# A decoder layer on one core: the expert blocks' tokens gathered from rows sorted once, in eight chunks, in place of a gather in every block

## What is computed

```
logits = rmsnorm(h) @ w_router + b_router          # 32 experts
top_v, top_e = top_k(logits, 4); gates = softmax(top_v)
for every expert e, x = the rows of rmsnorm(h) routed to e:
    gu   = x @ w_gate_up[e] + b_gate_up[e]          # 1024 -> 2048
    gate = min(gu[:, :1024], 7); up = clip(gu[:, 1024:], -7, 7)
    y    = ((up + 1) * gate * sigmoid(1.702 * gate)) @ w_down[e] + b_down[e]
    out[token] += gates[token, e] * y
```

## Time and profile before

| | us |
|---|---|
| median of 3 runs | 1140.28 (1140.24 to 1141.91) |
| profiled execution, its own time | 1138.94 |
| its span | 1137.1 |
| TensorE busy | 1101.7 (97%) |
| VectorE busy | 272.4 (24%) |
| ScalarE busy | 154.3 (14%) |
| moved by DMA | 427.34 MB, mean 376 GB/s |

### The profile page before, as it was taken

The page is one execution under the profiler, slowest core; times in us unless marked ns, Lnnn a source line. Parts: engine busy times, 40 slices in busy tenths (PEclk is TensorE's granted clock), DMA queues, the critical chain, the costliest instruction groups (busy, mean ns, idle before and its releaser), DMA issues.

```text
span 1137.1 us, 13236 instructions
## 1 busy us (share of the span) xinstructions
PE 1101.7 (97%) x5236; PEld 448.5 (39%) x5236; DVE 272.4 (24%) x623; ACT 154.3 (14%) x285; POOL 8.0 (1%) x28
## 2 busy tenths in 40 slices
PE   9999989999999999998999999999999999999997
PEld 7855755533333333333333333333333333333332
DVE  3643344421111111122111111111111111111111
ACT  3531323510000000010000000000000000000001
POOL 1000000000000000000000000000000000000000
PEclk9999998999999999999999999999999999999999
DMA  9593112899999999999999999999999999999996
GB/s 328 100 364 156 74 75 79 353 400 397 429 426 429 427 430 428 436 427 428 427 431 433 428 430 433 429 432 430 429 435 428 426 432 431 432 433 423 428 427 249
DMA packets 37329, 427.34 MB, mean 376 GB/s; under 512 B 6163, under 2 KB 8308, under 8 KB 17460
## 3 DMA queue, kind: packets, MB, share of 16 engines
q1 hardware_dynamic: 34724, 426.33, 89.7%
q10 hardware_dynamic: 2576, 0.59, 0.2%
HBM read 424.29 MB, written 2.62 MB: 375 GB/s over the span
## 4 chain that ended last, share of the span: by engine, by line
PE 80%; DMA 15%; ACT 2%; DVE 2%; issue 1%; SPq 0%; POOL 0%; ACTq 0%; DVEq 0%; POOLq 0%
PE bank L1677 31%; PE bank L1723 17%; DMA store<-in_w_gate_up_dram 8%; DMA store<-in_w_down_dram 7%; PE bank L1298 5%; PE bank L1619 4%; PE bank L1421 4%; PE bank L1305 4%; PE bank L1492 3%; PE bank L1369 2%; PE bank L1665 2%; PE bank L1608 2%; ACT conv L788 1%; PE bank L1685 1%; PE bank L1239 1%
## 5 line engine op out<-in xcount | busy, mean ns | idle before, releaser
L1677 PE MATMUL bank<-store,conv 128*64 128x512 f32 x2048 | 447.8, 595 | 1.5 <-DMA store<-in_w_gate_up_dram 1.5
L1677 PEld LDWEIGHTS bank<-store,conv 128*64 128x64 f32 x2048 | 144.1, 137 | 303.9 <-issue 296.9
L1723 PE MATMUL bank<-store,conv 128*64 128x512 f32 x1008 | 224.2, 595 | 5.9 <-DMA store<-in_w_down_dram 5.4
L1162 DVE TENSOR_SCALAR conv<-bank 128x512 f32<-128x512 f32 x32 | 22.1, 692 | 641.2 <-PE bank L1677 641.2
L1723 PEld LDWEIGHTS bank<-store,conv 128*64 128x64 f32 x1008 | 70.7, 137 | 137.7 <-issue 127.5
L782 ACT ACTIVATE conv<-conv 128x512 f32<-128x512 f32 x32 | 20.1, 629 | 497.6 <-DVE conv L1162 497.6
L1421 PE MATMUL bank<-arena,qkT 128*64 128x512 f32 x256 | 62.2, 605 | 0.2 <-DVE qkT L975 0.2
L1619 PE MATMUL bank<-qkT 64*128 64x512 f32 x248 | 61.6, 615 | 0.0
L1298 PE MATMUL bank<-store 128*128 128x512 f32 x128 | 56.4, 592 | 0.0
L792 ACT COPY qkT<-bank 128x512 f32<-128x512 f32 x32 | 18.7, 585 | 255.6 <-PE bank L1723 255.6
L1305 PE MATMUL bank<-store 128*128 128x256 f32 x192 | 42.7, 380 | 0.8 <-DVE store L842 0.8
(11 more groups left out here) (289 smaller groups left out, 578.2 us busy)
## 6 DMA issues: line engine op xcount, KB each, us to landing
store<-in_w_gate_up_dram SPq DMA_DIRECT2D x38, 4096.0 KB, 24.9
store<-in_w_down_dram SPq DMA_DIRECT2D x62, 2048.0 KB, 17.7
store<-in_w_gate_up_dram SPq DMA_DIRECT2D x52, 2048.0 KB, 16.5
store<-in_w_in_dram SPq DMA_DIRECT2D x7, 2048.0 KB, 22.8
store<-in_w_out_dram SPq DMA_DIRECT2D x1, 4096.0 KB, 18.0
extra<-in_w_down_dram SPq DMA_DIRECT2D x1, 2048.0 KB, 19.4
store<-in_w_down_dram SPq DMA_DIRECT2D x2, 1024.0 KB, 34.6
bias_by_distance<-extra SPq DMA_DIRECT2D x1, 1536.0 KB
```

The source lines that it names most:

```text
L1162: dve.tensor_scalar(gt, bank[4][:], LIMIT, None, ALU.min).then_inc(g_min, 1)
L1677: ins = mm(dst[SLOTS * hf:SLOTS * (hf + 1), :], xgT[:, c:c + SLOTS], store[:, slot_at(k, odd) + c0:slot_at(k, odd) + c0 + 512], start=Fals ...
L1723: ins = mm(dst[SLOTS * hf:SLOTS * (hf + 1), :], turned[:, c:c + SLOTS], w[:, hf * 512:(hf + 1) * 512], start=f == 0, stop=f == KT - 1)
```

## The change

All 1024 routed rows are put into their experts' order once, in a buffer in SBUF (`flow`, which also holds `hx`, `extra` and the old `conv`), turned and scaled. A block then takes its 64 columns from an offset that is read from a table (`win_at`).

- The buffer is filled by eight chunks of 128 rows. For each, VectorE makes two 0/1 matrices of 128x128 (`choose`), and TensorE multiplies the tokens `h` with them: 2 x 8 products of 128 columns (`chunk_half`). VectorE scales each half into place (`sorted_rows`, writing every eighth element). Chunks 0 and 1 are made in blocks 0 and 1, chunks 2 to 5 in blocks 2, 4, 6 and 8. Chunks 6 and 7 are made in `late_tables`, by two times 8 products of 256 columns (`chunk_end`), and TensorE waits there until VectorE has put them in place.
- `turns(b)` loses `gather`, the copy to `xg`, `gather_flip` and the scaling by VectorE. ScalarE copies the block's columns from `flow` to `xgT` (`window`).
- Block 0's rows are gathered already turned, by 16 products of 64 columns, so that ScalarE's norm of `h`, its copy and the transposes before block 0 go. The factor 1/rms is put into `SEL` and the chunk matrices.
- Five small products (`offsets`) inside block 0's `gate_up` sum the experts' counts to offsets.
- VectorE's loop over blocks 0 to 9 is written out.
- SyncE loads block 2's first down half ahead of block 1's second.

```diff
             for hf in range(2):
-                    if (m, hf) == (1, 0):
+                    if (m, hf) == (2, 0):
                         continue
-                    sp.wait_ge(wdn_used, 1 if hf == 0 else 2 * m)
-                    sp.dma_start(tile_dst(4 + hf), expert_tile(slice(m, m + 1), 4 + hf)).then_inc(ld_tile[4 + hf], 16)
+                    e = m if hf else 2
+                    sp.wait_ge(wdn_used, 2 * m if hf else 1)
+                    sp.dma_start(tile_dst(4 + hf), expert_tile(slice(e, e + 1), 4 + hf)).then_inc(ld_tile[4 + hf], 16)
...
+            def window(b):
+                at8 = act.value_load(win_at[0:1, bass.ds(b, 1)], min_val=0, max_val=KT * S * TOP_K)
+                act.wait_ge(wgu_used, 4 * b)
+                act.copy(xgT.rearrange("p (i h s) -> p i h s", i=4, h=2),
+                         flow[:, bass.ds(at8, KT * SLOTS)].rearrange("p (s h i) -> p i h s", h=2, i=4)
+                         ).then_inc(xgT_ready, 1)
...
+            def choose(chunk, dst):
+                if chunk:
+                    st.step(dve.tensor_scalar(pos4, pos4, -float(P), None, ALU.add))
+                both(lambda t: dve.tensor_scalar(dst[t], iota_p[:], pos4[:, 4 * t:4 * t + 1], None, ALU.is_equal))
+                for k in range(1, TOP_K):
+                    both(lambda t: dve.scalar_tensor_tensor(out=dst[t], in0=iota_p[:],
+                                                            scalar=pos4[:, 4 * t + k:4 * t + k + 1], in1=dst[t],
+                                                            op0=ALU.is_equal, op1=ALU.add))
                 for t in range(T):
+                    cr.mark(dve.tensor_scalar(dst[t], dst[t], nrm[:, 1, 2 + t:3 + t], None, ALU.mult))
...
+            def sorted_rows(at, n, k0, ks, src):
+                xs.mark(dve.tensor_tensor(
+                    flow[:, KT * at:KT * (at + n)].rearrange("p (s k) -> p k s", k=KT)[:, k0:k0 + ks],
+                    src[:].rearrange("p (k s) -> p k s", k=ks), wide(w2p[:, k0:k0 + ks], n), ALU.mult))
...
+                if chunk is not None:
+                    dve.wait_ge(ch_psum, 2 * chunk + 1)
+                    sorted_rows(P * chunk, P, 0, 4, bank[6])
                 dve.wait_ge(actT_psum, b + 1)
                 dve.tensor_copy(actT_last if last else actT, bank[4][:]).then_inc(actT_ready, 1)
-                if not last:
-                    dve.wait_ge(xgT_psum, b + 2)
-                    turned_rows().then_inc(xgT_ready, 1)
...
+            def chunk_half(c, half):
+                if half == 0:
+                    pe.wait_ge(chosen_ready, T * c + T)
+                if not (isinstance(c, int) and (c, half) == (0, 0)):
+                    pe.wait_ge(xs_ready, 2 * c + half)
+                for i in range(4):
+                    for t in range(T):
+                        ins = mm(bank[6][:, i * P:(i + 1) * P], h_rows(t, 4 * half + i), chosen[t], start=t == 0,
+                                 stop=t == T - 1)
+                ins.then_inc(ch_psum, 1)
...
+                pe.wait_ge(tab_ready, 10)
+                chunk_end(range(4, KT))
+                pe.wait_ge(xs_ready, 16)
...
-            def turns(b):
+            def turns(b, chunk=None):
                 turn_gates(b)
-                pe.wait_ge(S_ready, b + T + 1)
-                gather(0)
-                gather(1).then_inc(xg_psum, 1)
+                if chunk is not None:
+                    chunk_half(chunk, 0)
                 turn_act(b)
-                pe.wait_ge(xg_ready, b + 2)
-                gather_flip()
...
-            def rest(b):
-                turns(b)
+            def rest(b, chunk=None):
+                turns(b, chunk)
                 down(b, 0)
+                if chunk is not None:
+                    chunk_half(chunk, 1)
                 down(b, 1)
```

More of the change, by code:

```diff
@@ L263, in hybrid_layer @@
         rmT = conv[0:N_EXP, HG + T:HG + 2 * T, 0:P]
-        more, end, beg = (col[0:N_EXP, c:c + 1] for c in (24, 25, 26))
+        more, end, beg, cnt, extra_at = (col[0:N_EXP, c:c + 1] for c in (24, 25, 26, 27, 28))
+        minus_one = col[0:N_EXP, 3:4]
+        within, beyond = (tables[:, 192 + P * i:192 + P * (i + 1)] for i in range(2))
+        win_of, jump = r3[:, 448:480], r3[:, 480:512]
+        at = [left[t][:, 0:N_EXP] for t in range(T)]
+        pos4 = nrm[:, 7, 8:16]
         bank = [ctx.enter_context(nc.psum_tensor(f"bank{i}", [P, 512], F32)) for i in range(8)]
@@ L796, in expert_block @@
                 evacuate(b)
+                window(b + 1)
                 output(b, bank[7])
-            with act.Fori(0, FINE_BLOCKS) as b:
-                expert_block(b)
+            act.wait_ge(pad_ready, 1)
+            act.wait_ge(win_ready, 1)
+            with act.Fori(0, FINE_BLOCKS // 2) as pair:
+                for i in range(2):
+                    gated(2 * pair + i)
+                    evacuate(2 * pair + i)
+                    act.wait_ge(xs_ready, 2 * pair + (2 * i + 2))
+                    window(2 * pair + (i + 1))
+                    output(2 * pair + i, bank[7])
             act.wait_ge(gT_psum, 1)
@@ L1145, in _ @@
             shares(1)
[L1147 to L1156 removed]
+            dve.wait_ge(cnt_psum, 1)
@@ L1198, in _ @@
                 (st.step if j < S // SLOTS - 1 else nb.mark)(ins)
+            for c in range(2):
+                choose(6 + c, [chosen_end[t][:, P * c:P * (c + 1)] for t in range(T)])
             dve.wait_ge(end_psum, 1)
@@ L1601, in _ @@
             keep_clock()
-            pe.wait_ge(hn_ready, T)
             pe.wait_ge(S_ready, T)
-            gather(1).then_inc(xg_psum, 1)
-            def gather_flip():
-                for c in range(4):
-                    last = tp(bank[6][:, c * P:(c + 1) * P], xg_rows[:, c], ident[:])
-                last.then_inc(xgT_psum, 1)
-            pe.wait_ge(xg_ready, 1)
-            gather_flip()
+            gather(1).then_inc(xgT_psum, 1)
+            for t in range(T):
+                ins = mm(bank[1][0:N_EXP, 64:65], mask[t], ones[:, 0:1], start=t == 0, stop=t == T - 1,
+                         skip_group_check=True)
@@ L1614, in combine, with chunk_end @@
+            def chunk_end(ks):
+                for k in ks:
+                    dst = bank[(6, 7, 4, 5)[k // 2]][:, (k % 2) * S:(k % 2 + 1) * S]
+                    for t in range(T):
+                        ins = mm(dst, h_rows(t, k), chosen_end[t], start=t == 0, stop=t == T - 1)
+                ins.then_inc(ch_psum, 1)
             def combine(first=False, final=False):
@@ L1625, in late_tables @@
             def late_tables():
-                for i in range(T):
-                    ins = mm(bank[4][0:N_EXP, 0:1], mask[i], ones[:, 0:1], start=i == 0, stop=i == T - 1)
-                Tally(pe, cnt_psum).mark(ins)
                 pe.wait_ge(gates_ready, T)
@@ L1680, in gate_up @@
                         ins.then_inc(wgu_used, 1)
+                    if first and k == 1:
+                        offsets()
             def turn_gates(b, dst=bank[7]):
```

168 lines of the change are left out of this document (106 added, 62 removed).

## The result

| | before | after |
|---|---|---|
| median, us | 1140.26 (4 runs, 1139.86 to 1141.91) | 1196.74 (4 runs, 1193.53 to 1198.51) |
| ratio | | 1.0489 [1.0464, 1.0514] |
| span of the profiled execution | 1137.1 | 1194.5 |

The change costs 56.5 us where the prediction had 24 and ended its range at 1176. The direction was right, the size was not.

What follows compares the result with a forecast made beforehand. The prediction held the weight stream nearly full and TensorE's arrival at block 12's load decisive. Its terms 0.8 + 1.1 + 11.1 + 2.8 - 3.5 + 11.5 gave +23.8 us, forecasting 1164 us, range 1154 to 1176.

Steps and rivals of the forecast that it cites:

- way into block 0: Ahead of block 0, turned gathers replace the copy and transposes but take longer: +0.8 us.
- `offsets`: In block 0, five small products at 0.22 us each: +1.1 us (0.6 to 1.4).
- six blocks with a chunk: Chunk halves between `down` halves add 11.1 us; those in `turns` replace the gather but wait on VectorE, +2.8.
- four blocks without: Blocks 3, 5, 7, 9: the gather goes but VectorE's chain stays, saving 0.9 us of 1.89 each: -3.5 us.
- `late_tables` and the pause: Behind block 9: `chunk_end` products +7.1 us, then TensorE's wait for four `sorted_rows` +4.4: +11.5 us (9.7 to 12.9).
- half clock in block 6 and behind the tables: Only behind `late_tables`: a longer TensorE pause at half clock may add 0.6 us; not counted in the sum.
- block 12's load: Issued behind `late_tables`; each microsecond TensorE reaches its releasing product later is one of the result: +23.8 us.
- The step that failed: Chunk halves: 16 records at 1.85 us despite weights read every fourth element; 2.8 each only as upper end.
- The rule that I weighed: Chunk products' weights: a stride up to 16 bytes, four fp32 elements, is free, so 1.85 us a half stays.
- moved load: Block 2's first down half, loaded earlier, fills the dent at 255 us, but the gap returns at block 12's load: 0.
- the gather had been cover: In blocks without a chunk, the removed gather mostly covered VectorE's chain: only 0.9 us saved of 1.89.
- new wait: Rival: in blocks 0 and 1 `window` waits for the chunk's second half, or VectorE stalls: 1180 us, chance 0.10.

Runs made afterwards that it cites:

- unit rows: Changed kernel with token rows read side by side, weights left as they were, so the output differs: 1165.87 us, ratio 1.0230.
- experiment 2: Small program with only groups of 16 products or transposes at several weight pitches; 128 columns: 3.76 us at pitch 2, 7.36 at pitch 4.
- pitch-2 kernels: Changed kernel with rows of h paired, so product weights have a stride of 2 elements: 1172.74 us; the same without chunks 6 and 7: 1161.8 us.
- experiment 5: Kernel before with 28 idle products added ahead of block 10: 1148.04 us; or added behind block 27 instead: 1149.26 us.

## Why the prediction was wrong

Its sum and what the trace of after has, from the starts of `gate_up` (L1797: 237.75, 271.85, 305.62, 339.47, 366.10, and so on) against those of before:

| term | summed | measured |
|---|---|---|
| way into block 0 | +0.8 | 237.75 - 230.50 = +7.2 |
| `offsets` | +1.1 | +1.0 |
| six blocks with a chunk | +11.1 + 2.8 = +13.9 | 6 x 6.3 = +37.7 |
| four blocks without | -3.5 | 4 x -0.9 = -3.6 |
| `late_tables` and the pause | +11.5 | 25.7 - 13.9 = +11.8 |
| half clock in block 6 and behind the tables | 0 | 1.6 + 1.3 = +2.9 |
| block 12's load | +23.8 | +57.0 (timeline 57.2) |

- **The step that failed** is "I keep 1.85 since the records of L1608 still follow each other closely, and the ratio for the upper end". A chunk half takes 3.84 us on the average, and each gather 3.7 to 3.8. Six halves between the `down` halves and six in `turns` are 12 x 2.0 = 24 us above the sum; the second kind was summed as lying in the gather's place, which holds only at 1.85. Against the kernel with unit rows the two gathers add 3.7 us and their half clock about 2.0; the other 0.8 of the way into block 0 was missing from the sum without any pitch. The half clock in block 6 adds 1.6, `chunk_end` 0.8. L1608 was a bad witness: it is a transpose, one record, and in experiment 2 a transpose at this pitch costs 9% more, two records of a product of 128 columns twice as much. Why a transpose's load is the shorter one no run shows.
- **The rule that I weighed** was read too quickly, and the row that spoke against it, the longer load of L1608, was set aside. The Trainium skill (SBUF — State Buffer, "Door 1: The DMA port swizzle") says that a stride is free up to four fp32 elements, and in the same place that at least two accesses must fall in a 16-byte line. The trace of experiment 2 agrees with the second and not with the first: at pitch 2 (two accesses a line) 3.76 us, at pitch 3 5.52, at pitch 4 (one) 7.36, at pitch 8 (one) 7.51. That the line is the cause is that page's; the runs show only the steps.
- **Right:** the rule on block 12's load (later by 57.2, 24.2 and 10.5 us in three kernels, spans longer by 57.4, 23.7 and 10.3; in the pitch-2 kernels the span grows by 2.0 more than the load's shift, by their slower stream); the blocks of 26.6 us without a chunk; `sorted_rows` at 1.08 (1079 ns); `late_tables` (its chunks taken out: 10.9 for 11.5); that the moved load is worth nothing and its dent returns in part; that the gather had been cover, 0.9 saved of 1.9.
- **Half right:** the half clock. The prediction had 0.6 behind the tables as a possibility; it was 1.3 there, and came at two more places. `window` takes 1127 ns and still lies beside `down`: no new wait appeared in blocks 0 and 1.
- **Range:** the upper end of 1175 put the ratio of 1.5 on the six halves between the `down` halves alone. The gathers and the halves in `turns` have the same weights and had no such price. With a doubling of all fourteen groups it would have been 14 x 1.9 = 27 us above the sum, still without the half clock.

Not settled: why executions reach block 0 at different times though nothing ahead of it was changed. Its bias products start between 229.5 and 232.2 us in the kernels made from the one before, so one pair of executions can differ by 2.7 us for that alone.

## To carry to other kernels

Before a product takes its weights at a pitch, measure that very form, with its columns: at 64 and 128 columns a pitch of four elements doubled its time, at 512 it was free, and pitch 2 was nearly free everywhere. Where two resources are both full, find the one load behind which the queue runs dry and cost every edit as a shift of it; work that is removed ahead of it counts only as far as nothing else was waiting in its place, and work that is added behind it was not free here either (experiment 5). Where two profiled executions are compared, look first at when each reaches the part that was changed. Work that fills a pause may also keep the clock up: take it out and look at the granted clock, not only at the waits.

## What was not expected of the hardware

- The pace of these pitched weight loads does not follow TensorE's clock. In experiment 2 the group of 64 columns at pitch 4 took 7.36 us with the clock at half for its last third, exactly as the group of 128 columns at full clock, and the gathers of the kernel after took 3.81 us, with the clock falling, and 3.69 at half clock, the chunk halves 3.74 to 3.93 at full. The stretches of experiment 2:

```profile
238.00:240.00 2.00, 2.00 (x10) 2.00 (x10) 0.00 (x0) 1.00 0.00 0
240.00:242.00 2.00, 2.00 (x10) 2.00 (x10) 0.00 (x0) 0.85 0.00 0
242.00:244.00 2.00, 2.00 (x10) 2.00 (x10) 0.00 (x0) 0.50 0.00 0
244.00:246.00 2.00, 2.00 (x6) 1.64 (x6) 0.00 (x0) 0.50 0.00 0
```

- The clock can fall in the middle of such a group, though TensorE shows as busy throughout; its weight loads (the second busy time of each row) are busy for nearly all of it too, and that it waits for them is my reading. It need not fall: the group of 128 columns at pitch 4 kept full clock. The idle products behind the first group took 12.52 us instead of 10.36. In the kernel after the clock falls with the gathers at 226 us, and with unit rows it doesn't.
- In the kernel without gathers, with two pauses of about 1 us in each block, the clock fell in about every third block; with 1.3 us of idle products in them it did not fall in any block ahead of the tables, and behind block 10 once, at 998 us.
- Packets of 8 KB per partition gave 423 to 424 GB/s, 16 KB 428, and 32 KB 430.
